# The first projections regrouped: quarters of q, k and v, weights prepared ahead, gated attention's turns

## The chip, the cores and the metric

The kernel runs on one core of one Trainium2 chip. The metric is the device time of one execution in microseconds. Three executions of the kernel before took 2640.57, 2635.28 and 2639.64 us; the median is 2639.64.

## What is computed

The reference is two transformer blocks over 256 tokens of width 2048, all in float32. The diff touches the front of the first block only:

```python
mod = (silu(c) @ ada_w + ada_b)              # 6 x 2048: shift, scale, gate of the mixer and of the ffn
h = rmsnorm(x, norm_mix_g) * (1 + scale_m) + shift_m
(p_q, p_k, p_v, p_g, p_gk, p_cq, p_ckv, p_kr, p_ga, p_gb) = split(h @ w_in)
log_a = log_sigmoid(p_gk @ gla_gk_w + gla_gk_b) / 16
o = gla_chunked(q, k, v, log_a)              # gated linear attention, 4 heads
o = rmsnorm(o, gla_onorm_g) * silu(p_g)
y_gla = o @ gla_wo
# MLA attention from p_cq, p_ckv, p_kr; merged = sigmoid(p_ga) * y_gla + sigmoid(p_gb) * y_mla
```

Then come `w_out`, a gated FFN, and a second block of two layers, none of which the diff touches.

## The kernel before

**Matrix products.** Every weight is read once, in chunks of 128 x 2 x 512 floats (0.524 MB, two tiles of K). A product in float32 is made of three matmuls in fp32r: ScalarE copies the chunk to fp32r (`whi`), VectorE subtracts to get the rest (`wlo`), and TensorE multiplies whi with h's high part, wlo with h's high part and whi with h's low part, in `unit`. Both copies have four slots (`NW`), so the copy of weights chunk w + 4 waits until TensorE is done with chunk w. A product ("job") runs its chunks into one of two pairs of PSUM banks, in turn, and is then read out by `evac`, on ScalarE or VectorE.

**ada_w** doesn't go to TensorE as a matrix: VectorE adds each of its chunks, times a column of silu(c), to `acc` (12 groups of 16 chunks, `adas`). `ada_mod` then sums `acc` over the partitions with 16 one-column matmuls, and VectorE makes the scales `modc`. The mixer's shift and scale come from groups 0 to 3, each for one quarter of the 2048 features.

**The quarters.** h can be made for one quarter of the features when one ada_w group is summed. So q, k and v are computed in four quarters of K, and each later quarter is added to QT, KT or V (`adds`, in `evac` on VectorE, two instructions each). `quarters` in `make_jobs` holds the jobs. Before: in each quarter q and k (two jobs each, 4 tiles of K); v0 in quarter 0, v0 and v1 in quarter 1, and so on, so that a new column block of v starts with each quarter from K = 0. `units` is the order of all chunks: the 16 chunks of ada group 0, then for each of three quarters the 16 chunks of the next ada group, spread evenly, with the quarter's weights in its last 0.8. SP loads the chunks in this order, into 5 slots of raw and, up to here, 6 more (`NFIRST` is 11); each slot is loaded again as soon as VectorE has read it.

**The order of work.** `make_timeline` writes out one list that all engines follow, each picking its own parts. For each chunk of `units` it first emits `prep` for the chunks up to `LOOK` = 3 ahead, ada_w's counted, then the matmuls (`unit`), `evac` at a job's end, and then one step of each running helper stage (`stage_steps`). `until` runs stages on until a named step is out. An engine executes its parts strictly in that order. Stages that matter here: `start` (row sums and norm of X, on ScalarE, VectorE and POOL), `adaf` (`ada_mod`), `fnorm` (`fn_T`, the turn of X on TensorE, with ScalarE's scaling to `hraw`; `fn_hi`, rounding to h's high part on ScalarE and subtraction on VectorE), `tables` (angles, sines), `gk` (the gate's logarithm), `gla` (gated attention: 48 steps of scores, then `gla_av`, 8 products with v, and `gla_og`, 8 steps of turns), `lat` (latents of MLA), `pair` (its heads, two at a time, with softmax). `BORDERS` names jobs before which the tiles of h that they need must be out ahead of any further `prep`.

**The quarters' end.** In quarter 3 the jobs are gk, q, k, v0 to v3; `gla` is launched at v0 and must be out before `ygla` 0.

Of the kernel before, what the change touches and what calls it, by code (L numbers as in the profile page):

```python
# [149 lines left out]
BORDERS = [("fg", 0), ("rvg", 1, 0), ("q", 0, 0), ("q", 0, 1), ("q", 0, 2), ("gk",)]  # L150
# [19 lines left out]
def make_jobs(I):  # L170
# [33 lines left out]
    for qd in range(4):  # L204
        if qd == 3:
            job = gemm("gk", (), lambda k: [(half, sl, cols(w_in, k + 4 * half, o, n, 4)) for half in range(2)
                                            for sl, o, n in ((slice(0, 64), o_kr, 64), (slice(64, 80), o_gk, 16))], KD, 80, "h", turned=True, kn=8)
            quarters[3].append(job)
        for kind, o in (("q", o_q), ("k", o_k)):
            for j in range(2):  # L210
                quarters[qd].append(gemm(kind, (j, qd) if qd < 3 else (j,), wcols(w_in, o + 512 * j, 512), 4, 512, "h", turned=True, k0=4 * qd,
                                         adds=(kind, j, qd - 1) if qd else None))
        for j in range(qd + 1):
            k0 = 0 if j == qd else 4 * qd
            quarters[qd].append(gemm("v", (j, qd) if qd < 3 else (j,), wcols(w_in, o_v + 512 * j, 512), 4 * qd + 4 - k0, 512, "h", k0=k0,
                                     adds=("v", j, qd - 1) if k0 else None))
# [2537 lines left out]
```

## Time and profile before

| | us |
|---|---|
| median of three executions | 2639.64 (2635.28 to 2640.57) |
| span of the profiled execution, first to last instruction | 2637.0 |
| TensorE busy | 2552.6 (97%) |
| VectorE busy | 1699.4 (64%) |
| ScalarE busy | 1281.6 (49%) |

The profile is of one execution; its time is known as its span, and the median of the executions stands 2.6 us above that. PE is TensorE's matmuls, PEld its weight loads, DVE VectorE, ACT ScalarE, POOL GpSimd, SP the engine that issues most loads. `gp` are the PSUM banks of the products, `tp` those of the helper steps. L830, L1270, L1884, L1887 and L1890 are lines of small helpers (matmul, activation, tensor_tensor, tensor_scalar, scalar_tensor_tensor) through which most work is issued, so the tiles tell which step a row belongs to. "x" is a count of instructions; in the rows of groups the mean is that of one instruction.

### The profile page before, as it was taken

Reading aid. Unit: us, or ns where it says so; the run is one execution under the profiler, and the core shown is the slowest. Engines: PE = TensorE matmul, PEld = TensorE weight load, DVE = VectorE, ACT = ScalarE, POOL = GpSimd, SP = SyncE. Lnnn points to the kernel's source line nnn. Section 1 sums busy time; section 2 is a strip of 40 time slices with the busy share of each in tenths; the row PEclk is TensorE's granted clock in tenths of the full one; section 3 lists DMA queues with packets and bytes.
Section 4 is the critical chain, followed back from the end, with each engine's and each line's share of the span. In section 5 each row is a group of like instructions: output and inputs, shape, how many; then the busy total and the mean of one; then the engine's idle time right before and its main releaser. Section 6 shows DMA issues by size and latency. Waiting matters only on the chain.

```text
span 2637.0 us, 33987 instructions
## 1 busy us (share of the span) xinstructions
PE 2552.6 (97%) x12327; PEld 2145.5 (81%) x12327; DVE 1699.4 (64%) x2194; ACT 1281.6 (49%) x1824; POOL 63.1 (2%) x102
## 2 busy tenths in 40 slices
PE   3889999999999999999999999999999999999999
PEld 3878887888887887888888888889888887888887
DVE  6887776776676765566655545565666655676664
ACT  3345455444555444544443444455754545565553
POOL 0000000000000000000000000000000100010000
PEclk9999999999999999999999999999999999999999
DMA  9975665898676665687756666566665465665564
GB/s 364 346 258 152 185 207 183 284 313 269 205 246 200 232 204 187 218 279 253 258 191 194 190 191 190 181 191 181 187 187 172 135 219 147 184 187 180 149 199 135
DMA packets 279920, 555.73 MB, mean 211 GB/s; under 512 B 24286, under 2 KB 45100, under 8 KB 279116
## 3 DMA queue, kind: packets, MB, share of 16 engines
q1 hardware_dynamic: 274048, 541.79, 64.6%
q0 software_dynamic: 3040, 8.69, 1.0%
q10 hardware_dynamic: 2668, 3.09, 0.3%
q8 instruction: 100, 1.64, 0.3%
q14 instruction: 64, 0.52, 0.1%
HBM read 549.83 MB, written 2.10 MB: 209 GB/s over the span
## 4 chain that ended last, share of the span: by engine, by line
PE 91%; DVE 4%; ACT 2%; issue 1%; DMA 1%; SPq 0%; POOL 0%; DVEq 0%; ACTq 0%
PE gp L830 83%; PE tp L830 5%; PE tp L833 2%; DMA raw_first<-in_ada_w_dram 1%; DVE wlo L1884 1%; ACT whi L1270 1%; DVE acc L1890 1%; DVE xs L1884 0%; SPq L813 0%; ACT hraw L1270 0%; DVE stat L2208 0%; ACT sx L1270 0%; DVE sx L1884 0%; DVE yd L1884 0%; ACT h L1270 0%
## 5 line engine op out<-in xcount | busy, mean ns | idle before, releaser
L1884 DVE TENSOR_TENSOR wlo<-raw,whi 128x1024 fp32r<-128x1024 f32 (+1 forms) x830 | 986.0, 1197 | 690.1 <-ACT whi L1270 687.4
L830 PE MATMUL gp<-whi,h 128*128 128x512 f32 (+1 forms) x4352 | 1371.4, 389 | 7.5 <-DVE wlo L1884 4.8
L1270 ACT ACTIVATE whi<-raw 128x1024 fp32r<-128x1024 f32 (+1 forms) x830 | 851.0, 1037 | 666.9 <-PE gp L830 545.6
L830 PEld LDWEIGHTS gp<-whi,h 128*128 128x128 f32 x4352 | 815.6, 188 | 165.9 <-issue 14.0
L830 PE MATMUL gp<-wlo,h 128*128 128x512 f32 (+1 forms) x2176 | 834.8, 384 | 0.0
L830 PEld LDWEIGHTS gp<-wlo,h 128*128 128x128 f32 x2176 | 409.9, 188 | 72.7 <-issue 1.7
L1890 DVE SCALAR_TENSOR_TENSOR acc<-raw,cact,acc 128x1024 f32<-128x1024 f32 x149 | 190.6, 1279 | 7.0 <-DMA raw<-in_ada_w_dram 6.2
L830 PE MATMUL gp<-whi,ah 128*128 128x512 f32 x352 | 137.9, 392 | 0.0
L830 PE MATMUL gp<-whi,al 128*128 128x512 f32 x352 | 137.1, 389 | 0.0
L830 PE MATMUL gp<-wlo,ah 128*128 128x512 f32 x352 | 136.9, 389 | 0.0
L830 PE MATMUL gp<-h,whi 128*128 128x256 f32 (+1 forms) x528 | 106.2, 298 | 20.9 <-ACT whi L1270 10.7
L830 PEld LDWEIGHTS gp<-h,whi 128*128 128x128 f32 (+1 forms) x528 | 87.6, 200 | 25.6 <-issue 16.0
L830 PE MATMUL gp<-whi,mxh 128*128 128x512 f32 x256 | 99.8, 390 | 0.0
L830 PE MATMUL gp<-whi,mxl 128*128 128x512 f32 x256 | 99.6, 389 | 0.0
L830 PE MATMUL gp<-wlo,mxh 128*128 128x512 f32 x256 | 99.6, 389 | 0.0
L830 PE MATMUL gp<-h,wlo 128*128 128x256 f32 (+1 forms) x272 | 79.2, 291 | 0.0
L830 PEld LDWEIGHTS gp<-whi,al 128*128 128x128 f32 x352 | 66.1, 188 | 13.9
L830 PEld LDWEIGHTS gp<-whi,ah 128*128 128x128 f32 x352 | 66.1, 188 | 13.4
L830 PEld LDWEIGHTS gp<-wlo,ah 128*128 128x128 f32 x352 | 66.1, 188 | 13.4
L2603 POOL TENSOR_TENSOR stat<-stat,cst 128x2 f32<-128x2 f32 (+1 forms) x37 | 30.1, 816 | 1436.6 <-DVE stat L1887 1436.4
L1270 ACT ACT_TABLE_LOAD x44 | 56.5, 1283 | 6.2 <-issue 2.9
L830 PEld LDWEIGHTS gp<-wlo,mxh 128*128 128x128 f32 x256 | 48.1, 188 | 10.0
(331 smaller groups left out, 2593.7 us busy)
## 6 DMA issues: line engine op xcount, KB each, us to landing
raw<-in_w_in_dram SPq DMA_DIRECT2D x310, 512.0 KB, 4.3
raw<-in_ffn_w_in_dram SPq DMA_DIRECT2D x176, 512.0 KB, 4.5
raw<-in_ada_w_dram SPq DMA_DIRECT2D x158, 512.0 KB, 4.8
raw<-in_w_out_dram SPq DMA_DIRECT2D x96, 512.0 KB, 4.4
raw<-in_ffn_w_down_dram SPq DMA_DIRECT2D x88, 512.0 KB, 4.3
raw<-in_w_in_dram SPq DMA_DIRECT2D x64, 384.0 KB, 3.3
raw_first<-in_ada_w_dram SPq DMA_DIRECT2D x34, 512.0 KB, 8.4
raw<-in_gla_wo_dram SPq DMA_DIRECT2D x32, 512.0 KB, 5.8
```

The source lines that it names most:

```text
L830: return e.matmul(o, l, r, start=start, stop=stop)
L833: return e.transpose(o, i, ident[0:n, 0:n])
L1270: return e.activation(o, i, f, **kw)
L1884: return e.tensor_tensor(o, a, b, op)
L1890: return e.scalar_tensor_tensor(out=o, in0=a, scalar=s, in1=b, op0=op0, op1=op1)
L2603: e.tensor_tensor(dst, dst, cst[:, C_HALF:C_HALF + n], ALU.pow).then_inc(pow_out, 1)
```

## The change

1. **The quarters.** Quarter 0: q, k over K tiles 0 to 3, v0 over 0 to 3. Quarter 1: no q or k; v1, v2, v3 over tiles 0 to 7. Quarter 2: q, k and v0 over 4 to 11. Quarter 3: v2 over 8 to 15, gk, q and k over 12 to 15, v3 and v1 over 8 to 15, v0 over 12 to 15. 13 partial additions in place of 18. The first halves of v2 and v3 are kept in `VPART`, since X still stands where V will be; `gk_la` waits until v2 is added, since `VPART[2]` lies in LOGA.
2. **The start.** The first two weights chunks stand right behind ada group 0. `x_ss` comes two steps earlier; the turn of X for the first quarter belongs to `start` and precedes `ada_mod`; what ScalarE did in `fn_T` is now `fn_mod`, VectorE's subtraction is `fn_lo`, a step of its own from quarter 1 on. `adaf` 0 and `fnorm` 0 are emitted ahead of the last two ada chunks of group 0. `BORDERS` keeps only the first of the quarters.
3. **Ahead.** From the last chunk of ada group 0 on, `prep` runs to three weights chunks ahead, ada_w's not counted.
4. **The tables** are launched after `fnorm` 3, not 2; `gla` at v3, which is now the first job after k.
5. **Gated attention.** Four of the eight `gla_og` steps stand between the `gla_av` steps, each needing its own head only; `ygla` asks for the tiles that it reads, not for all of `gla`; `lat` needs the last `gla_av` (`GLA_AV`).

```diff
-BORDERS = [("fg", 0), ("rvg", 1, 0), ("q", 0, 0), ("q", 0, 1), ("q", 0, 2), ("gk",)]
+BORDERS = [("fg", 0), ("rvg", 1, 0), ("q", 0, 0)]
+GLA_AV = ("gla", 63)
...
-    for qd in range(4):
...
-        for kind, o in (("q", o_q), ("k", o_k)):
-            for j in range(2):
-                quarters[qd].append(gemm(kind, (j, qd) if qd < 3 else (j,), wcols(w_in, o + 512 * j, 512), 4, 512, "h", turned=True, k0=4 * qd,
-                                         adds=(kind, j, qd - 1) if qd else None))
-        for j in range(qd + 1):
-            k0 = 0 if j == qd else 4 * qd
...
+    qk(0, None, 0, 4)
+    value(0, 0, None, 0, 4)
+    for j in range(1, 4):
+        value(1, j, None, 0, 8)
+    qk(2, 0, 4, 8)
+    value(2, 0, 0, 4, 8)
+    value(3, 2, 1, 8, 8)
...
+    qk(3, 2, 12, 4)
+    value(3, 3, 1, 8, 8)
+    value(3, 1, 1, 8, 8)
+    value(3, 0, 2, 12, 4)
...
-        spots = [((i + 0.5) / 16, 0, u) for i, u in enumerate((adas[qd + 1], ci) for ci in range(KD))]
-        spots += [(0.2 + 0.8 * (i + 0.5) / len(mine), 1, u) for i, u in enumerate(mine)]
+        lead = mine[:2] if qd == 0 else []
+        units += lead
+        mine = mine[len(lead):]
+        spots = [((0.9,1,1)[qd] * (i + 0.5) / 16, 0, u) for i, u in enumerate((adas[qd + 1], ci) for ci in range(KD))]
+        spots += [(0 + (1 - 0) * (i + 0.5) / len(mine), 1, u) for i, u in enumerate(mine)]
...
-        return [idle] * 2 + [step(("x_sq", (), 0)), step(("rows", (), 1))] + [idle] * 4 + [step(("x_ss", (), 0)), idle] + \
-            [step(("x_norm", (t,), 0)) for t in range(2)]
+        return [idle] * 2 + [step(("x_sq", (), 0)), step(("rows", (), 1)), idle, idle, step(("x_ss", (), 0)), idle] + \
+            [step(("x_norm", (t,), 0)) for t in range(2)] + [step(("fn_T", (0,), 1), ("fn_T", (1,), 1))]
...
-        return [step(("fn_T", (2 * j,), 1), ("fn_T", (2 * j + 1,), 1), need=[("start",)]),
-                step(("fn_hi", (2 * j,), 0), ("fn_hi", (2 * j + 1,), 0), *([("gla_loads", (), 0)] if j == 3 else no))]
+        turn = [step(("fn_T", (2 * j,), 1), ("fn_T", (2 * j + 1,), 1))] if j else []
...
-        steps += [step(("gla_av", (h, t), 1), need=[("evac", "v", 3), ("evac", "g", h)]) for h in range(4) for t in range(2)]
-        return steps + [step(("gla_og", (k,), 1)) for k in range(0, KD, 2)]
+        for h in range(4):
+            for t in range(2):
+                turn = [("gla_og", (4 * h + 2 * t - 6,), 1)] if 2 * h + t in (3, 4, 5, 6) else []
+                steps += [step(("gla_av", (h, t), 1), *turn, need=[("evac", "v", 0), ("evac", "g", h)])]
+        return steps + [step(("gla_og", (k,), 1)) for k in range(8, KD, 2)]
...
-                if sid == ("fnorm", 2):
+                if sid == ("fnorm", 3):
                     launch("tables")
...
-        while prep < min(n + LOOK + 1, len(chunks)):
+        ahead = weights_at[n] + LOOK
+        while prep < len(chunks) and (prep <= n + LOOK if n < KD - 1 else prep <= n or weights_at[prep] <= ahead):
...
+        if n == KD - 2:
+            launch("adaf", 0)
+            until(("fnorm", 0))
...
-                if job["name"] == ("ygla", 0):
-                    until(("gla",))
...
-                if job["name"] == ("v", 0):
+                if job["name"] == ("v", 3):
                     launch("gla")
...
+    VPART = {2: w1("vpart2", 0, [2, 512]), 3: w1("vpart3", 42.5, [2, 512])}
...
         def gk_la(us, t):
             for n, u in enumerate(us):
+                w.wait_ge(gp_dve[job_of["v", 2]["no"] % 2], at("gpd", "v", 2))
...
-            for h in range(4):
-                for t in range(2):
-                    taken_dve(first_use("gla_av", h, t))
+            for t in range(2):
+                taken_dve(first_use("gla_av", k // 4, t))
```

## Rows read from the trace of the kernel before

**Rows 1.** The page: span, and busy time of each engine.
```profile
span 2637.0 us, 33987 instructions
PE 2552.6 (97%) x12327; PEld 2145.5 (81%) x12327; DVE 1699.4 (64%) x2194; ACT 1281.6 (49%) x1824; POOL 63.1 (2%) x102
```

**Rows 2.** Busy time by stretch; columns: length, busy, granted clock, DMA share, GB/s.
```profile
0.00:48.80 48.80, 6.36 (x27) 5.42 (x27) 26.88 (x28) 14.55 (x18) 4.97 (x11) 1.00 1.00 356
48.80:83.10 34.30, 31.50 (x219) 29.73 (x219) 27.41 (x24) 12.02 (x16) 0.00 (x0) 1.00 1.05 386
83.10:90.30 7.20, 2.63 (x25) 2.39 (x23) 4.94 (x9) 6.00 (x11) 0.00 (x0) 0.78 1.01 373
90.30:134.20 43.90, 43.70 (x283) 40.09 (x283) 40.52 (x43) 12.47 (x13) 0.00 (x0) 0.96 0.95 329
134.20:152.60 18.40, 11.74 (x81) 11.36 (x79) 13.83 (x28) 10.67 (x16) 0.00 (x0) 0.81 0.68 226
...
48.80:197.20 148.40, 133.75 (x858) 122.46 (x859) 124.85 (x152) 57.89 (x74) 0.00 (x0) 0.95 0.90 313
197.20:300.00 102.80, 99.70 (x589) 86.22 (x587) 76.03 (x99) 52.36 (x71) 0.61 (x2) 0.98 0.55 165
...
700.00:900.00 200.00, 192.09 (x949) 161.37 (x948) 142.79 (x230) 107.55 (x187) 0.96 (x2) 1.00 0.69 221
```

**Rows 3.** TensorE in order of time, start: start us, us, operation, [idle before].
```profile
37.32 3.58 PE L830 MATMUL tp<-cst,acc 128*128 128x1 f32 x16 [17.88 <-DVE acc L1890]
40.76 1.95 PE L833 MATMUL tp<-cst,xs 128*128 128x128 f32 x8
```

**Rows 4.** ScalarE and VectorE in order of time, 33 to 50 us.
```profile
33.69 3.90 ACT L1270 ACTIVATE xs<-xs,stat 128x2048 f32<-128x2048 f32 x2 [12.61 <-POOL stat L2603]
...
38.81 1.29 DVE L1890 SCALAR_TENSOR_TENSOR acc<-raw_first,cact,acc 128x1024 f32<-128x1024 f32 x1 [0.69 <-DMA raw_first<-in_ada_w_dram]
...
42.30 1.28 DVE L1890 SCALAR_TENSOR_TENSOR acc<-raw_first,cact,acc 128x1024 f32<-128x1024 f32 x1 [2.21 <-DMA raw_first<-in_ada_w_dram]
43.51 0.15 DVE L1890 SCALAR_TENSOR_TENSOR modc<-tp,gcol 128x4 f32<-128x4 f32 x1
...
43.90 1.93 ACT L1270 ACTIVATE hraw<-tp,modc 128x256 f32<-128x256 f32 x4 [6.31 <-DVE modc L1884]
...
46.65 1.15 ACT L1270 ACTIVATE h<-hraw 128x512 fp32r<-128x512 f32 x2
...
48.02 1.29 DVE L1884 TENSOR_TENSOR h<-hraw,h 128x512 fp32r<-128x512 f32 x2
```

**Rows 5.** Chain that ended last, 0 to 300 us: start us, us, what.
```profile
48.85 7.82 PE gp L830 x48
...
152.58 8.88 PE gp L830 x72
...
192.64 1.68 PE tp L830 x16
...
239.19 2.73 PE gp L830 x12
```

**Rows 6.** Waits of TensorE, 48.8 to 197.2 us: total, times, longest.
```profile
PE gp L830 <- DVE wlo L1884: 10.0, 8, 5.6
```

**Rows 7.** DMA queues besides SP's, 0 to 200 us: packets, MB, share.
```profile
q10 hardware_dynamic: 2668, 3.09, 4.4%
q0 software_dynamic: 304, 0.66, 0.9%
```

**Rows 8.** VectorE's groups, 48.8 to 197.2 us: count, busy us, mean ns, idle before.
```profile
L1890 DVE SCALAR_TENSOR_TENSOR acc<-raw_first,cact,acc 128x1024 f32<-128x1024 f32 x22 | 28.2, 1280 | 0.3
L1884 DVE TENSOR_TENSOR wlo<-raw_first,whi 128x1024 fp32r<-128x1024 f32 x22 | 26.8, 1221 | 6.8 <-ACT whi L1270 6.8
...
L1884 DVE TENSOR_TENSOR qt<-gp,qt 128x512 f32<-128x512 f32 x8 | 5.1, 684 | 2.3 <-PE gp L830 2.3
```

**Rows 9.** Waits of TensorE, 700 to 900 us: total, times, longest.
```profile
PE gp L830 <- DVE wlo L1884: 4.9, 6, 1.6
```

More of the change, by code:

```diff
@@ L321, in stage_steps @@
         (j,) = args
-        return [step(("fn_T", (2 * j,), 1), ("fn_T", (2 * j + 1,), 1), need=[("start",)]),
-                step(("fn_hi", (2 * j,), 0), ("fn_hi", (2 * j + 1,), 0), *([("gla_loads", (), 0)] if j == 3 else no))]
+        turn = [step(("fn_T", (2 * j,), 1), ("fn_T", (2 * j + 1,), 1))] if j else []
+        last = [("gla_loads", (), 0)] if j == 3 else []
+        return turn + [step(*[(part, (2 * j + n,), 0) for n in range(2) for part in ("fn_mod", "fn_hi")], *([("fn_lo", (2 * j + n,), 0) for n in range(2)] if j == 0 else []), *last)] + \
+            ([step(*[("fn_lo", (2 * j + n,), 0) for n in range(2)])] if j else [])
     if kind == "tables":
@@ L338, in stage_steps @@
             steps += [step(("gla_qk", x, 0), *[("gla_diff", y, 0) for y in ahead]), step(*[("gla_exp", y, 0) for y in ahead]), step(("gla_sc", x, 1))]
-        steps += [step(("gla_av", (h, t), 1), need=[("evac", "v", 3), ("evac", "g", h)]) for h in range(4) for t in range(2)]
-        return steps + [step(("gla_og", (k,), 1)) for k in range(0, KD, 2)]
+        for h in range(4):
[3 more added lines that the diff above has]
+        return steps + [step(("gla_og", (k,), 1)) for k in range(8, KD, 2)]
     if kind == "lat":
         (name,) = args
-        return [idle, idle, idle, step(("lat_T", (name, 0), 1), need=[("gla",)]), step(("lat_T", (name, 2), 1))]
+        return [idle, idle, idle, step(("lat_T", (name, 0), 1), need=[GLA_AV]), step(("lat_T", (name, 2), 1))]
     if kind == "pair":
@@ L471, in stat_need @@
             return [("ffn", k // 2 + 1)]
+        if s == "og":
+            return [("gla", 59 + k // 2)] if k < 8 else [("gla", 60 + k // 2)]
         if s in ("lq", "lk"):
@@ L489, in stat_need @@
         return []
-    prep = 0
+    weights_at, prep = [0], 0
+    for c in chunks:
+        weights_at.append(weights_at[-1] + c["gemm"])
+    late = {1, 2, 3}
     launch("start")
@@ L503, in make_timeline @@
                 was = j["seq"] - (2 if j["seq"] < 4 else 1)
+                if was in late:
+                    late.remove(was)
+                    launch("adaf", was)
                 if was >= 0:
@@ L509, in make_timeline @@
             prep += 1
-        if job["kind"] == "ada" and ci == KD - 1 and job["seq"] < 4:
+        if n == KD - 2:
+            launch("adaf", 0)
+            until(("fnorm", 0))
+        if job["kind"] == "ada" and ci == KD - 1 and job["seq"] in late:
+            late.remove(job["seq"])
             launch("adaf", job["seq"])
@@ L1390, in norm_hi, with fn_mod @@
             note(h_hi, "h", was, pair)
-        def fn_T(us, pair):
+        def fn_mod(us, pair):
             m = first_use("ada_mod", pair // 2)
             w.wait_ge(tp_dve[m.b], at("tpd", *m))
-            norm_T(us[0], pair, hraw, 1, 0, "h")
+            norm_T(first_use("fn_T", pair), pair, hraw, 1, 0, "h")
         def fn_hi(us, pair):
@@ L1762, in evac @@
             elif kind == "v":
-                read(first_use("fn_T", 2 * args[0]))
-                read(first_use("fn_T", 2 * args[0] + 1))
+                j = args[0]
+                if j in VPART:
+                    w.wait_ge(ss_done, at("ss", "x_ss"))
+                else:
+                    read(first_use("fn_T", 2 * j))
+                    read(first_use("fn_T", 2 * j + 1))
                 for n in range(2):
-                    copy(V[:, n, args[0] * 512:(args[0] + 1) * 512], ps[n][:, :]).then_inc(gp_act[g], 1)
+                    copy(VPART[j][:, n, :] if j in VPART else V[:, n, j * 512:(j + 1) * 512], ps[n][:, :]).then_inc(gp_act[g], 1)
             elif kind == "g":
@@ L1987, in norm_lo, with fn_lo @@
             tt(HL[:, kt, :], hr[:, pair % 2, :, :], HH[:, kt, :].bitcast(F32), ALU.subtract).then_inc(h_lo, 1)
-        def fn_hi(us, pair):
+        def fn_lo(us, pair):
             norm_lo(pair, hraw, "h")
@@ L2171, in gla_og @@
             gains()
-            w.wait_ge(ss_done, at("ss", "gla_av", 3, 1))
+            if k >= 8:
+                w.wait_ge(ss_done, at("ss", "gla_av", 3, 1))
             lo_pair(us[0], OGH, OGL, k, [gc(G_ON + (k + n) % 4) for n in range(2)])
@@ L2519, in evac @@
                 if kind == "v":
-                    to = V[:, :, args[0] * 512:(args[0] + 1) * 512]
+                    j = args[0]
+                    to = V[:, :, j * 512:(j + 1) * 512]
+                    if j in VPART:
+                        read(first_use("fn_T", 2 * j))
+                        read(first_use("fn_T", 2 * j + 1))
                     for n in range(2):
-                        tt(to[:, n, :], ps[n][:, :], to[:, n, :], ALU.add).then_inc(gp_dve[g], 1)
+                        tt(to[:, n, :], ps[n][:, :], (VPART[j] if j in VPART else to)[:, n, :], ALU.add).then_inc(gp_dve[g], 1)
                 else:
```

23 lines of the change are left out of this document (12 added, 11 removed).

## The prediction

> **What bounds the kernel now.** I read the page first: TensorE is busy 2552.6 of 2637.0 us [rows 1]. The change issues the same matmuls and transposes on the same operands, so it can win only what the other 84.4 us hold, plus what a throttled clock costs. Then the busy time by stretch [rows 2]: 42.4 us of TensorE's idle time lie before 48.8 us, where the first ada_w group is loaded and the first normed quarter is made; 14.7 us between 48.8 and 197.2, where the quarters of q, k and v run; 3.1 us from there to 300; 7.9 us between 700 and 900, where the pairs of heads run. The rest of the span holds 16.4 us, at places that the diff doesn't touch. In the quarters the mean granted clock is 0.95. Full speed is 2.4 GHz, the lower level half of it, so about a tenth of these 148.4 us ran at half speed: its worst pieces are 83.1 to 90.3 (0.78) and 134.2 to 152.6 (0.81), each just after TensorE had stood idle.
>
> What TensorE waits for in the quarters is prepared weights: ten microseconds for `wlo` in eight places [rows 6]. The two worst places are the borders between quarters. There the last ada_w chunk of the old quarter is summed, TensorE makes its columns (`ada_mod`, 1.68 us [rows 5]), VectorE the scales, TensorE turns X, ScalarE scales and rounds, VectorE subtracts: one chain, with nothing of the new quarter that TensorE could run beside it.
>
> DMA is full in the first quarter, 386 GB/s at a share of 1.05 [rows 2]. It is ahead, though. By 83.1 us it had moved 356 GB/s x 48.8 us + 386 GB/s x 34.3 us = 30.6 MB; 3.75 MB of that are other queues' [rows 7]; 26.9 MB are 51 chunks of 0.524 MB, while TensorE had then used chunk 42. One chunk takes 0.524 MB / 386 GB/s = 1.36 us.
>
> **The change part by part.** *The start.* `x_ss` stands two idle steps earlier, that is two ada_w chunks, at least 2 x 1.36 us: ScalarE's norm of X ends at 34.9 at the latest instead of 37.6 [rows 4]. TensorE's turn of X (1.95 us [rows 3]) then ends by 36.9, ahead of `ada_mod` (37.32, 3.58 us [rows 3]), where today it follows it. Two weights chunks stand behind ada group 0, and VectorE does their `wlo` before the scales. Chunk 17 was there at 38.81 [rows 4]; copy and subtraction of it end near 41.0, the end of `ada_mod` too. From there 0.4 us of scales (43.51 to 43.90), 1.93/2 of `hraw`, 1.15/2 of `h`, 1.29/2 of the subtraction [rows 4]: first matmul at 43.8 instead of 48.85, a gain of 5.0. If chunk 17 lands as late as chunk 18 did (42.30 [rows 4]) it is 47.3, a gain of 1.5.
>
> *Quarter 0.* 8 chunks of q and k at 8.88/3 = 2.96 us and 2 of v at 2.73 [rows 5] are 29.1 us; the first two ran at the low clock and took 7.82 instead of 5.92 [rows 5], which I keep: 43.8 + 29.1 + 1.9 = 74.8. Its last chunk (index 41) lands at 83.1 - 9.2 x 1.36 = 70.6, in time.
>
> *Quarter 1* now is v1 to v3 alone over 8 tiles of K: 12 chunks of v, 16 of ada_w, no partial addition. TensorE needs 12 x 2.73 + 1.68 + 1.0 (two turns at full speed, an estimate from half of 1.95) = 35.4 us, VectorE 16 x 1.28 + 12 x 1.22 = 35.1 [rows 8], DMA 28 x 1.36 = 38.1. So DMA sets the end: chunk 69 lands at 83.1 + 18.8 x 1.36 = 108.7; copy, subtraction and 2.73 of matmuls make it 113.6. The border is covered by two chunks of v1 that need only the first normed quarter. VectorE's scales stand behind every chunk prepared ahead (through index 50, which lands at 82.5), so normed tiles come at 86, TensorE is there at 83.3 and waits 2.7 us; supply hides that.
>
> *Quarter 2* has 8 tiles of K for q, k and v0: 16 x 2.96 + 4 x 2.73 = 58.3 us of TensorE for 36 chunks, 49.0 us of DMA: TensorE sets the pace. At its border the scales wait behind index 77 (119.6), the normed tiles come at 123.5, TensorE is there at 122.1: 1.4 us. 113.6 + 1.7 + 1.0 + 58.3 + 1.4 = 176.0. For the clock after these waits I add 1.7 us, about half of what 134.2 to 152.6 lost (18.4 x 0.19). The quarters end at 177.7 where they now end at 197.2: **-19.5**, of which the start is a quarter. Ends of this term: with no wait, TensorE's work alone, 171.0 (-26); with the start at 47.3, DMA at 329 GB/s as from 90.3 to 134.2 [rows 2] and both border costs as now, -10. I stay near the first: in the stretch before it DMA gave 386 GB/s, and nothing is added to what it must bring.
>
> *Five partial additions fewer.* Each is two instructions of 0.684 us [rows 8], 6.8 us of VectorE. I cost them at nothing by themselves: the VectorE time of quarter 1 above is already without them, and supply is slower. Without that cover they would be worth 6.8 us at most. Quarter 3 now has eight additions for seven; 1.4 us of VectorE, hidden by 24 chunks of TensorE.
>
> *The tables* (some 6 us of VectorE) are launched a quarter later. They now sit in the worst stretch, 134.2 to 152.6; in quarter 3 VectorE is busy 76.0 of 102.8 us [rows 2]. The steps of gk stand behind them, and `gk_la` also waits on ScalarE for the addition of v2, with the copies of weights queued behind it; but v2 was added some four chunks before, and gla starts only with v3, eight chunks of q and k after gk. SP's queue carries the same loads in the new order, POOL's the same steps (its loads for gla still stand with the last normed quarter). **0**, from -4 (the 3.1 us idle and the clock of 0.98 go) to +3 (the wait moves there).
>
> *Three weights chunks ahead, ada_w's not counted.* Before, an ada_w chunk among the next three leaves two weights chunks, 5.5 us of cover. Where chunks alone fill the ring nothing changes. Between 700 and 900 bursts of VectorE and ScalarE work for the softmax hold back `wlo`: 4.9 us in six waits, none over 1.6 [rows 9]. A further chunk covers 2.1 to 2.8 us, more than any of them. **-4**, of 7.9 idle; from -7 to +3, since the softmax's own steps now stand behind one more chunk.
>
> *Gated attention turned as it ends.* Eight turns of 4 transposes each move from behind the last `gla_av` to between them, and ygla no longer waits for all of gla. TensorE does the same work, and the stretch after 197.2 shows next to no idle time outside those named. **0**, +-1.
>
> Sum: -19.5 - 4 = -23.5 on a span of 2637.0, 2613.5; the median run is 2.6 us above the span, which I keep: **2616.1**.
>
> **The skill against a row.** DMA moved 386 GB/s over 34 us [rows 2]. The Trainium skill, "DMA: Bandwidth & Descriptors", section Specifications, puts HBM's limit for a core at about 358 GB/s. By it 70 chunks and 3.75 MB are there at 113.0 us, quarter 1 ends at 117.9, and the sum is 2620.4; the row says that a core which runs alone gets more.
>
> **The rivals.** (1) *The supply is later than I count* (0.17): the weights of v1 to v3 arrive behind ada_w chunks, quarter 1 stalls as the borders do now, and the clock falls. For it: slack of 0 to 3 us on three resources at once in quarter 1. Against it: DMA was nine chunks ahead. That is the -10 end, with -2 elsewhere: 2627. The skill's limit, above, is a mild form of it. (2) *All of it comes through* (0.12): -26 and -7, 2606. (3) *Slower: helper steps too late* (0.06). Between 300 and 900 each ScalarE or VectorE step of gla and of the pairs now stands behind the preparation of a third weights chunk, which waits for the slot that TensorE just left. If a pair's chain pays for this twice, 8 pairs x 2 x 2.1 us = 34 us come back: 2650. It decides from the point where such a step takes longer than the two chunks (5.5 us) that are left ahead of TensorE. Against it: stretches without ada_w work this way already, and at the present spacing TensorE waits little there for anything but `wlo`. (4) *Nothing in the end* (0.09): the quarters finish earlier, but gla, whose first steps wait for k, the tables and the gate, then sets the pace before v is done: 2637. Against it: gla's start keeps its distance from gk, and TensorE has ten chunks of quarter 3 and all of g beside it.
>
> **How the numbers follow.** Forecast 0.56, at 2616 (2609 to 2624 with the bounds of its terms). Range 2605 to 2632: it takes in the forecast, (1) and most of (2). A measurement of this kernel tells 0.2%, 5 us, from no change. Faster: the forecast, (1), (2), 0.85; same: (4), 0.09; slower: (3), 0.06.
>
> **What would show it.** First gp matmul at 43 to 45 us. No stretch of the quarters with a clock below 0.9, and no idle piece of TensorE over 3 us in them. The last `ada_mod` of the quarters near 173 instead of 192.64 [rows 5]. 700 to 900, counted from its own start, with 3 to 5 us idle. Wrong if the first matmul is at 47 or later, if quarter 1 ends after 118, if the profile shows TensorE waiting for `tp` steps of the pairs by over 5 us in sum, or if the gain before gla is given back before ygla.

## The result, and the profile after

The changed kernel takes 2614.39 us (median; 2612.94 to 2616.49), the kernel before beside it 2639.77: a ratio of 0.9909, 95% interval 0.9897 to 0.9921. The forecast was 2616, within 2605 to 2632. The total is right to 1.6 us. Its terms aren't: they miss by up to 5 us and cancel. Of one version below, the changed kernel without the look-ahead, one execution of four was in a slow state (3225.19 us, at a mean clock of 0.753), and its times are those of the other three.

The page of the changed kernel, as in [rows 1]: span, and busy time of each engine.

```profile
span 2614.7 us, 34013 instructions
PE 2546.4 (97%) x12327; PEld 2142.6 (82%) x12327; DVE 1697.4 (65%) x2184; ACT 1289.7 (49%) x1824; POOL 62.2 (2%) x102
```

TensorE has the same 12327 matmuls, VectorE ten instructions fewer. Lines L861 and L864 are now the matmul helper, L1300 ScalarE's, L1919, L1922 and L1925 VectorE's. The span fell by 22.3 us, the median by 25.4. The difference lies in which execution was profiled: each of the changed kernel's four takes 1.8 us more than its own span, and the profiled one (2616.49) is the slowest of them. So the median stands 0.3 us below the profiled span, where before it stood 2.6 above.

Busy time by stretch, as in [rows 2] (length, then PE, PEld, DVE, ACT, POOL busy, granted clock, DMA share, GB/s). The first three are quarter 0, quarter 1, and the time until TensorE has done 792 matmuls into `gp`, a count that [rows 2]'s kernel reached at 197.2.

```profile
46.30:82.00 35.70, 33.93 (x241) 32.31 (x242) 32.69 (x29) 14.95 (x20) 0.00 (x0) 1.00 1.05 386
82.00:119.70 37.70, 34.44 (x147) 28.01 (x145) 34.60 (x34) 18.74 (x25) 0.00 (x0) 0.95 1.05 387
119.70:182.70 63.00, 62.61 (x482) 60.51 (x481) 50.61 (x54) 29.36 (x35) 0.00 (x0) 1.00 0.85 295
...
700.00:900.00 200.00, 196.20 (x963) 165.00 (x962) 142.15 (x220) 108.92 (x180) 0.96 (x2) 1.00 0.68 221
```

The stretches with a clock near 0.8 have no like here: up to matmul 792 the clock is low once, for 3.4 us from 91.3, where before it was low twice for 6.8 (from 87.1 and 138.3). But three resources are now close to full in quarters 0 and 1 at once: TensorE idles 1.8 and 3.3 us, VectorE is busy 32.7 of 35.7 and 34.6 of 37.7 us (27.4 of 34.3 in quarter 0 before), and DMA stands at a share of 1.05 for 73 us. ScalarE shows what that means: between 46 and 182 us it waits for DMA in 22 places.

Waits of ScalarE in the changed kernel, 46 to 182 us (total, times, longest):

```profile
ACT whi L1300 <- DMA raw_first<-in_w_in_dram: 24.1, 12, 3.7
ACT whi L1300 <- DMA raw<-in_w_in_dram: 17.5, 10, 4.3
```

TensorE in order of time, the idle pieces over 0.33 us from 34 to 240 us (start, us, operation, [idle before]); [rows 3] shows the first two of before.

```profile
34.01 1.97 PE L864 MATMUL tp<-cst,xs 128*128 128x128 f32 x8 [14.83 <-ACT xs L1300]
38.25 3.54 PE L861 MATMUL tp<-cst,acc 128*128 128x1 f32 x16 [2.27 <-DVE acc L1925]
46.30 0.55 PE L861 MATMUL gp<-h,whi 128*128 128x256 f32 x1 [4.50 <-DVE h L1919]
...
65.94 0.36 PE L861 MATMUL gp<-h,whi 128*128 128x256 f32 x1 [0.35 <-DVE wlo L1919]
...
69.66 0.35 PE L861 MATMUL gp<-h,whi 128*128 128x256 f32 x1 [0.61 <-DVE wlo L1919]
...
73.57 0.47 PE L861 MATMUL gp<-whi,h 128*128 128x512 f32 x1 [0.80 <-DVE wlo L1919]
...
90.74 0.47 PE L861 MATMUL gp<-whi,h 128*128 128x512 f32 x1 [3.26 <-DVE h L1919]
...
128.62 0.36 PE L861 MATMUL gp<-h,whi 128*128 128x256 f32 x1 [0.39 <-DVE h L1919]
...
223.91 0.39 PE L861 MATMUL gp<-h,whi 128*128 128x256 f32 x1 [2.46 <-DVE qt L1919]
```

The two border waits of the kernel before, which [rows 6] don't tell apart:

```profile
90.34 0.55 PE L830 MATMUL gp<-h,whi 128*128 128x256 f32 x1 [4.60 <-ACT whi L1270]
...
140.61 0.55 PE L830 MATMUL gp<-h,whi 128*128 128x256 f32 x1 [5.59 <-DVE wlo L1884]
```

The turn stands ahead of `ada_mod` as foretold, at 34.01 instead of 40.76 [rows 3]; the first product starts at 46.30 instead of 48.85 [rows 5]. Of the borders between the quarters one wait of size is left in this profile, at 90.74; a second profile of the same kernel, below, has two of about 2 us. The last `ada_mod` of the quarters runs at 174.5, where it ran at 192.64 [rows 5].

To place the gain I counted TensorE's matmuls into `gp` in both traces and compared when each count is reached. At the first product the changed kernel is 2.6 us ahead; at the 792nd (197.2 before, 182.7 now) 14.5; after gated attention (1900 matmuls) 16.9; after the pairs (3400) 22.3, and about as much at the end. So: **quarters with the start -14.5, quarter 3 and gated attention -2.4, pairs -5.4**. Below, "at matmul 792" is this count.

### The profile page after: what moved, and what is told of

It reads as the page before. It is cut to its first block, busy times and chain, and to the rows that moved or that the text cites. A ratio compares the mean times of both kernels' runs of the same rounds, so it can differ in the third digit from the quotient of the medians.

```text
span 2614.7 us, 34013 instructions
## 1 busy us (share of the span) xinstructions
PE 2546.4 (97%) x12327; PEld 2142.6 (82%) x12327; DVE 1697.4 (65%) x2184; ACT 1289.7 (49%) x1824; POOL 62.2 (2%) x102
## 4 chain that ended last, share of the span: by engine, by line
PE 87%; DVE 2%; ACT 1%; issue 1%; POOL 0%; DVEq 0%; ACTq 0%
PE gp L861 79%; PE tp L861 5%; PE tp L864 2%; DVE wlo L1919 0%; ACT whi L1300 0%; DVE xs L1919 0%; DVE stat L2244 0%; DVE yd L1919 0%; ACT sx L1300 0%; DVE rg L1925 0%; DVE sx L1919 0%; DVE sx L1922 0%; DVE st L1919 0%; ACT mxh L1300 0%; DVE stat L1922 0%
## 5 line engine op out<-in xcount | busy, mean ns | idle before, releaser
L1919 DVE TENSOR_TENSOR wlo<-raw,whi 128x1024 fp32r<-128x1024 f32 (+1 forms) x828 | 987.0, 1197 | 703.5 <-ACT whi L1300 700.7
L861 PE MATMUL gp<-whi,h 128*128 128x512 f32 (+1 forms) x4352 | 1368.4, 389 | 7.1 <-DVE h L1919 4.9
L1300 ACT ACTIVATE whi<-raw 128x1024 fp32r<-128x1024 f32 (+1 forms) x828 | 854.3, 1036 | 770.7 <-PE gp L861 705.9
L861 PEld LDWEIGHTS gp<-whi,h 128*128 128x128 f32 x4352 | 815.5, 188 | 160.8 <-issue 10.8
L861 PE MATMUL gp<-wlo,h 128*128 128x512 f32 (+1 forms) x2176 | 834.5, 384 | 0.0
L861 PEld LDWEIGHTS gp<-wlo,h 128*128 128x128 f32 x2176 | 410.0, 188 | 72.7 <-issue 1.2
L1925 DVE SCALAR_TENSOR_TENSOR acc<-raw,cact,acc 128x1024 f32<-128x1024 f32 x150 | 191.9, 1279 | 7.8 <-DMA raw<-in_ada_w_dram 6.7
L861 PE MATMUL gp<-whi,ah 128*128 128x512 f32 x352 | 138.0, 392 | 0.0
L861 PE MATMUL gp<-whi,al 128*128 128x512 f32 x352 | 137.1, 389 | 0.0
L861 PE MATMUL gp<-wlo,ah 128*128 128x512 f32 x352 | 137.0, 389 | 0.0
L861 PE MATMUL gp<-h,whi 128*128 128x256 f32 (+1 forms) x528 | 103.7, 294 | 8.5 <-DVE h L1919 4.9
L861 PE MATMUL gp<-whi,mxh 128*128 128x512 f32 x256 | 99.8, 390 | 0.0
L861 PE MATMUL gp<-whi,mxl 128*128 128x512 f32 x256 | 99.7, 389 | 0.0
L861 PE MATMUL gp<-wlo,mxh 128*128 128x512 f32 x256 | 99.6, 389 | 0.0
L861 PEld LDWEIGHTS gp<-h,whi 128*128 128x128 f32 (+1 forms) x528 | 85.6, 196 | 12.4 <-issue 8.3
L861 PE MATMUL gp<-h,wlo 128*128 128x256 f32 (+1 forms) x272 | 78.3, 288 | 0.0
L861 PEld LDWEIGHTS gp<-whi,al 128*128 128x128 f32 x352 | 66.1, 188 | 13.9
L861 PEld LDWEIGHTS gp<-wlo,ah 128*128 128x128 f32 x352 | 66.1, 188 | 13.5
L861 PEld LDWEIGHTS gp<-whi,ah 128*128 128x128 f32 x352 | 66.1, 188 | 13.4
L861 PEld LDWEIGHTS gp<-wlo,mxh 128*128 128x128 f32 x256 | 48.1, 188 | 10.0
```

Source lines behind the costliest of these rows:

```text
L861: return e.matmul(o, l, r, start=start, stop=stop)
L1300: return e.activation(o, i, f, **kw)
L1919: return e.tensor_tensor(o, a, b, op)
L1925: return e.scalar_tensor_tensor(out=o, in0=a, scalar=s, in1=b, op0=op0, op1=op1)
```

## The experiments

The one-part versions come first, then the disputed costs, then what follows for a better kernel. Ratios are to the kernel before. No run turns back the new start alone, nor one part of the diff that neither the list of the change nor the forecast names: the new `spots` spread a quarter's weights over all of it, no longer over its last 0.8.

**Look-ahead alone, on the kernel before.**

```diff
-        while prep < min(n + LOOK + 1, len(chunks)):
+        ahead = weights_at[n] + LOOK
+        while prep < len(chunks) and (prep <= n + LOOK if n < KD - 1 else prep <= n or weights_at[prep] <= ahead):
```

> The kernel before with one part of the change alone: from the last chunk of ada group 0 on, three weights chunks are prepared ahead, ada_w's not counted. Theory (three separate gains: the start 2.5 us, the covered borders and the new quarters some 14, the pairs 5): only the 0.6 to 0.8 us waits for wlo at job ends in the first quarter and the wlo waits between 640 and 940 us go, so 5 to 8 us under the kernel before, some 2632; no wait for wlo is left in the pairs, the two borders stay. Rival (looking further ahead is what counts, the regrouping is only a rearrangement): 17 us or more under, 2623 or less.

Measured: 2636.51 us, ratio 0.9995 (0.9986 to 1.0004): nothing that can be told from no change, and less than either theory had. Yet in its trace two things of opposite sign happened. In the pairs it gains 6.8 us by the count of matmuls. At the front it loses 10.5 us by the 96th matmul, 5.9 at matmul 792. ScalarE, VectorE and TensorE of this kernel, each in order of time, about its first product:

```profile
54.78 1.06 ACT L1273 ACTIVATE whi<-raw_first 128x1024 fp32r<-128x1024 f32 x1 [3.01 <-DMA raw_first<-in_w_in_dram]
...
57.08 0.15 DVE L1893 SCALAR_TENSOR_TENSOR modc<-tp,gcol 128x4 f32<-128x4 f32 x1
...
60.78 0.55 PE L833 MATMUL gp<-h,whi 128*128 128x256 f32 x1 [17.55 <-DVE h L1887]
```

`ada_mod` was done at 41.4, but the scales (`modc`) stand in VectorE's queue behind every chunk that is prepared ahead; the last of these landed at 54.78. So the look-ahead makes the chain longer at the start, and at the first border too (a wait of 6.14 us, before 4.60), but not at the second (5.41, before 5.59). It pays here only with the new start and the new jobs at the borders, which the next version shows from the other side.

**The changed kernel without the look-ahead.** The same line, turned back.

```diff
-        while prep < len(chunks) and (prep <= n + LOOK if n < KD - 1 else prep <= n or weights_at[prep] <= ahead):
+        while prep < min(n + LOOK + 1, len(chunks)):
```

> The changed kernel with the old look ahead (three chunks, ada_w's counted). Theory: the pairs lose their 5 us again, and in quarters 0 to 2 the waits for wlo come back in part, 1 to 4 us: 2620 to 2624; TensorE waits for wlo by some 5 us in the pairs. Rival (looking ahead counts for most): 2632 or more.

Measured: 2626.55, ratio 0.9956 (0.9939 to 0.9972), 12.2 us above the changed kernel, 9.5 by the span: between the theories. The old waits for `wlo` are back; waits of TensorE in this kernel, 46 to 190 us, then 700 to 900:

```profile
PE gp L860 <- DVE wlo L1918: 8.0, 8, 3.5
```
```profile
PE gp L860 <- DVE wlo L1918: 3.5, 4, 1.6
```

At matmul 792 it is 5.0 us behind the changed kernel, after gated attention 6.7, after the pairs 10.0. So the look-ahead gives 5 us in the quarters, 1.7 in quarter 3 and gated attention (2.6 in the experiment before this one), 3.3 in the pairs. What I put down to the regrouping is to a third the look-ahead's. In the pairs this kernel is still 2.0 us ahead of the kernel before, without the look-ahead; no run shows why.

**The changed kernel with the old quarters.** 18 additions, v column by column as before; start, look-ahead and turns as changed.

```diff
-    qk(0, None, 0, 4)
-    value(0, 0, None, 0, 4)
-    for j in range(1, 4):
-        value(1, j, None, 0, 8)
...
+    for qd in range(4):
+        for kind, o in (("q", o_q), ("k", o_k)):
...
+        for j in range(qd + 1):
```

> The changed kernel with the old quarters of q, k, v (18 partial additions, each quarter beginning with a chunk of q that needs the tiles normed last), everything else as changed. Theory: the borders are bare again, two to three of them at some 5 us of idle time and 2 to 3 us of low clock each: 10 to 15 us over the changed kernel, 2625 to 2630, with idle pieces of 4 us or more where quarters 1 and 2 begin. Rival (regrouping is worth nothing once weights are further ahead): within 3 us of the changed kernel, 2612 to 2618.

Measured: 2622.95, ratio 0.9942 (0.9927 to 0.9957): 8.6 us above the changed kernel, 5.6 by the span, 7.6 at matmul 792: again between the two. TensorE at its two borders:

```profile
87.76 0.55 PE L851 MATMUL gp<-h,whi 128*128 128x256 f32 x1 [6.29 <-DVE h L1908]
...
136.03 0.55 PE L851 MATMUL gp<-h,whi 128*128 128x256 f32 x1 [3.89 <-DVE h L1908]
```

Here q's first chunk needs the new normed quarter at once; in the changed kernel two chunks of v1 stand ahead of it. At each the clock was low for 6.8 us. These two places are where the trace shows the regrouping's gain, 5.6 to 8.6 us in all. (The spread of `spots` stayed as changed.)

**The five additions put back as bare VectorE time.** Ten 128 x 512 additions into a spare tile at the ends of v1, v2 and v3 of quarter 1; nothing else is touched.

```diff
+            if kind == "v" and len(args) == 2 and args[1] == 1:
+                w.wait_ge(d_first, at("first"))
+                w.wait_ge(mm_done, job["chunks"][-1]["w"] + 1)
+                for n in range(4 if args[0] < 3 else 2):
+                    tt(SPARE[:, :], cst[:, 0:512], cst[:, 512:1024], ALU.add).then_inc(dve_self, 1)
+                    w.wait_ge(dve_self, own())
+                return
```

> The changed kernel with the VectorE time of five partial additions put back: ten additions of 128 x 512 floats into a spare tile, 6.8 us in all, where the jobs of quarter 1 end (four behind v1, four behind v2, two behind v3). Nothing of the result hangs on them. Theory (the additions cost nothing by themselves): within 1.5 us of the changed kernel, 2613 to 2616. Rival (VectorE sets the pace of quarter 1, so its five additions fewer are the gain there): 5 to 7 us more, 2619 to 2621.

Measured: 2620.08, ratio 0.993 (0.9914 to 0.9947): 5.7 us above the changed kernel, 3.8 by the span, 3.5 at matmul 792. "Nothing by themselves" is wrong: the median lies in the rival's range, the trace below it. In this kernel, VectorE's spare additions from 85 to 130 us, and TensorE:

```profile
L1920 DVE TENSOR_TENSOR spare<-cst 128x512 f32<-128x512 f32 x10 | 6.9, 690 | 0.2
```
```profile
118.64 0.47 PE L862 MATMUL gp<-whi,h 128*128 128x512 f32 x1 [1.86 <-DVE wlo L1920]
...
132.09 0.36 PE L862 MATMUL gp<-h,whi 128*128 128x256 f32 x1 [2.06 <-DVE h L1920]
```

6.9 us of VectorE (idle for only 0.2 us ahead of them) in a stretch where it had 3.1 us to spare come out as two waits, 3.9 us together. Where I had taken nothing, they cost about half their time by the trace, in two profiles whose clock fell once each up to matmul 792 (against the repeat below, whose clock didn't fall, it is 5.1 us), and four fifths by the medians.

**The old turns of gated attention.**

```diff
-        for h in range(4):
-            for t in range(2):
-                turn = [("gla_og", (4 * h + 2 * t - 6,), 1)] if 2 * h + t in (3, 4, 5, 6) else []
...
+        return steps + [step(("gla_og", (k,), 1)) for k in range(0, KD, 2)]
```

> The changed kernel with gated attention's turns as before: all eight behind the last product with v, each waiting for all eight products, and ygla waiting for all of gla. Theory (the turns are TensorE's own work wherever they stand, and there is other work beside them): within 1.5 us of the changed kernel, 2613 to 2616; the stretch from quarter 3 to the first product of uq as long as in the changed kernel, within 0.8 us. Rival (the 2.6 us that the change gained between the end of quarter 2 and uq are the turns'): 2 to 3 us more, 2616.5 to 2617.5.

Measured: 2614.17, ratio 0.9904, span 2614.7. **The tables launched as before:**

```diff
-                if sid == ("fnorm", 3):
+                if sid == ("fnorm", 2):
                     launch("tables")
```

> The changed kernel with the tables launched when the third normed quarter is done, as before, not the fourth. Theory (some 6 us of VectorE come into quarter 2, where TensorE sets the pace, and leave quarter 3, where the gate's chain holds an addition of q back by 2.5 us): -2 to +2 us against the changed kernel, 2612 to 2616.5. Rival (moving the tables is worth the 2.6 us gained between quarter 2 and uq): 2 to 4 us more, with a new idle piece of over 1 us in quarter 2.

Measured: 2613.99, span 2613.0. Neither part's worth can be told from nothing, as forecast. The second shows more: the wait of 2.5 us in quarter 3 (222.21 there) doesn't come from the tables. ScalarE and VectorE of the changed kernel ahead of 223.91:

```profile
215.82 1.06 ACT L1300 ACTIVATE whi<-raw 128x1024 fp32r<-128x1024 f32 x1 [5.29 <-DMA raw<-in_w_in_dram]
216.90 1.28 ACT L1300 ACT_TABLE_LOAD   x1
218.19 2.19 ACT L1300 ACTIVATE loga<-loga,cst 128x1024 f32<-128x1024 f32 x2
...
221.43 1.23 DVE L1919 TENSOR_TENSOR wlo<-raw,whi 128x1024 fp32r<-128x1024 f32 x1 [0.83 <-ACT whi L1300]
222.57 1.28 DVE L1919 TENSOR_TENSOR qt<-gp,qt 128x512 f32<-128x512 f32 x2
```

ScalarE waited 5.29 us for the chunk of 215.82; the gate's table load and logarithm follow on ScalarE, the next copy stands behind them, and the addition of q, for whose banks TensorE waits, stands behind that copy's subtraction. As these rows read, the price sits in the order of the queues; no run changed that order.

**Scales one chunk earlier.** The prediction's start failed at the chunks that VectorE must subtract ahead of the scales. Here only one of them is left.

```diff
-        if n == KD - 2:
+        if n == KD - 3:
             launch("adaf", 0)
```

> The changed kernel with the first scales and the first normed quarter emitted one ada chunk earlier, so that VectorE has one weights chunk, not two, in front of them. Theory (the first matmul waits for the second of those two chunks, which landed at 41.06 us): first product at 45.0 instead of 46.3 us, and since quarter 1 waits for VectorE later anyway, 0 to 1.3 us less in all, 2613 to 2614.5. Rival (the first weights chunk itself is late, so that nothing changes, or the second one then is): first product at 46 or later, 2614 to 2616.

Measured: 2613.86; first product:

```profile
44.27 0.55 PE L861 MATMUL gp<-h,whi 128*128 128x256 f32 x1 [3.37 <-DVE h L1919]
```

2.0 us earlier than in the changed kernel. 0.9 of it isn't the edit's: the last ada_w chunk of group 0 came earlier in this execution, and `ada_mod` began at 37.35 instead of 38.25. The other 1.1 are the second chunk's. At matmul 792 the kernel is 1.7 us ahead of the first profile of the changed kernel and level with its repeat (below).

**v1 and v2 interleaved at the border of quarter 1**, so that four chunks, not two, need no new normed tile.

```diff
+        if qd == 1:
+            mine = [mine[i] for i in (0, 1, 4, 5, 2, 3, 6, 7, 8, 9, 10, 11)]
```

> The changed kernel with the chunks of quarter 1 in the order v1, v1, v2, v2 (first normed quarter), v1, v1, v2, v2 (second), then v3, so that four chunks and not two need no newly normed tile. Theory (TensorE's 3.3 us of idle time and the low clock behind it, 1.7 us, come from those scales standing on VectorE behind the chunks prepared ahead): no idle piece over 1 us and no low clock where quarter 1 begins, 2 to 5 us less, 2609.5 to 2612.5. Rival (VectorE sets the pace of quarter 1, so what isn't waited for there is waited for later): within 1.5 us of the changed kernel, with a new idle piece at the border to quarter 2.

Measured: 2615.69, ratio 0.9912. The wait at that border is gone, and one at the next has come:

```profile
126.93 0.36 PE L863 MATMUL gp<-h,whi 128*128 128x256 f32 x1 [2.71 <-DVE h L1921]
```

TensorE ended quarter 1 at 115.8, 0.7 us ahead of the repeat below, but the scales of the next border came no earlier (the product there starts at 126.93, in the repeat at 126.96), mostly as the rival had it. If cover helps, both borders need it.

**Half of ada_w's loads left out.** Groups 1 and 2 (those of quarters 0 and 1) are loaded half; all engines work as before.

```diff
-"src": [(slice(0, 512), src[k * P:(k + 1) * P])]
+"src": [(slice(0, 256), src[k * P:(k + 1) * P, :, 0:256]) if seq in (1, 2) else (slice(0, 512), src[k * P:(k + 1) * P])]
```

> The changed kernel, but the chunks of ada_w that stand in quarters 0 and 1 (groups 1 and 2) are loaded only half (256 of each 512 columns); the rest of the slot keeps old data, so these scales are not the reference's. VectorE, ScalarE and TensorE do all their work as before; 8.4 MB of 21 in these quarters are not moved. It tells whether the supply or VectorE sets the waits of quarters 0 and 1 in the changed kernel. Supply (my theory for quarter 0): the waits of 0.35 to 0.8 us in quarter 0 go, quarter 0 ends 1.5 to 2 us earlier, ScalarE's waits for DMA (24.1 us there) nearly go; at the border to quarter 1 VectorE is early too; the quarters end 4 to 6 us earlier, 2608 to 2611. Rival (VectorE, 92% busy in quarter 1, sets it): the quarters end within 1.5 us of the changed kernel, 2612.5 to 2615.

**Cover at both borders** (and the scales one chunk earlier):

```diff
-        if n == KD - 2:
+        if n == KD - 3:
...
+        if qd:
+            mine = [mine[i] for i in (0, 1, 4, 5, 2, 3, 6, 7)] + mine[8:]
```

> The changed kernel with the first scales emitted one ada_w chunk earlier, and with the jobs at both inner borders interleaved (v1 and v2 in quarter 1, the two q jobs in quarter 2), so that four chunks, not two, need only normed tiles that are there. Theory: the waits at the borders are a matter of cover; first product at 44.3 us, no idle piece over 1 us at either border, 4 to 6 us off: 2608.5 to 2611. Rival: supply and VectorE take back what the cover gives, some wait follows within the same quarter: 2612 to 2615.

**The changed kernel once more, beside these two.**

> The changed kernel itself once more, beside the two others on the same chip, as their yardstick: 2613 to 2616, first product at 46.3 us, border waits of 2 to 3.5 us where they fell before or at the next border.

Measured: half loads 2611.51 (0.9899; 0.9886 to 0.9913), cover at both 2612.04 (0.9900; 0.9887 to 0.9914), the changed kernel again 2615.47 (0.9913; 0.9900 to 0.9927). The repeat's waits at the two borders, then all waits of TensorE with half loads, 40 to 140 us, and its windows 46.3 to 82 and 82 to 119.7, the times of the changed kernel's quarters 0 and 1:

```profile
89.03 0.47 PE L861 MATMUL gp<-whi,h 128*128 128x512 f32 x1 [1.88 <-DVE h L1919]
...
126.96 0.36 PE L861 MATMUL gp<-h,whi 128*128 128x256 f32 x1 [2.08 <-DVE h L1919]
```
```profile
PE gp L861 <- DVE h L1919: 5.5, 2, 4.7
PE gp L861 <- DVE wlo L1919: 1.1, 2, 0.6
...
46.30:82.00 35.70, 34.62 (x244) 33.06 (x244) 34.56 (x31) 17.16 (x23) 0.00 (x0) 1.00 0.90 285
82.00:119.70 37.70, 36.84 (x182) 30.96 (x181) 37.28 (x39) 19.23 (x25) 0.00 (x0) 1.00 0.99 341
```

Half loads: neither theory whole. ScalarE's waits for DMA between 46 and 182 us fall from 41.6 us to 3.9, yet quarter 0 keeps two of its waits for `wlo` (0.47 and 0.61): with the data there, VectorE is busy 34.6 of 35.7 us and is the next limit. My theory for quarter 0 falls. At the borders it holds: the first wait shrinks to 0.86 (4.7 of the 5.5 is the start's) and the second is gone; the quarters reach matmul 792 at 177.6, against 181.1 in the repeat and 182.7 in the first profile. Supply is worth 3.5 us against the repeat, whose clock didn't fall up to there either, by the scales' and copies' queues; behind it VectorE has nothing left (37.3 of 37.7 us).

Cover at both borders: no idle piece over 0.7 us from 46 to 219 us, and matmul 792 at 178.4. The borders are as the theory said, the time isn't: it lies 3.4 us below the repeat in the median and 2.8 in the span, at the edge of the rival's range. The first product came at 45.26, not 44.3, and quarter 0 has four waits of 0.4 to 0.6 us, which take part of it back. It is the lowest of the kernels here that compute everything. The two intervals overlap, but each of its four executions (2609.69 to 2612.74) lies below each of the nine of the changed kernel (2612.94 to 2616.90), so a small gain is likely.

## Why the prediction came out, by its own steps

**The start: mis-sized.** Gain 2.55, not 5.0. ScalarE, then VectorE of the changed kernel, as in [rows 4]:

```profile
39.70 1.06 ACT L1300 ACTIVATE whi<-raw_first 128x1024 fp32r<-128x1024 f32 x1 [5.75 <-DMA raw_first<-in_w_in_dram]
41.06 1.06 ACT L1300 ACTIVATE whi<-raw_first 128x1024 fp32r<-128x1024 f32 x1 [0.30 <-DMA raw_first<-in_w_in_dram]
...
40.86 2.58 DVE L1919 TENSOR_TENSOR wlo<-raw_first,whi 128x1024 fp32r<-128x1024 f32 x2 [2.76 <-ACT whi L1300]
43.36 0.15 DVE L1925 SCALAR_TENSOR_TENSOR modc<-tp,gcol 128x4 f32<-128x4 f32 x1
```

The step took chunk 17's landing from before, 38.81 [rows 4]; it landed at 41.06. From the end of its subtraction to the first product the forecast had 2.8 us (the items that it names add up to 2.6), measured 2.9. Only the landing failed, inside the bounds given (43.8 to 47.3). One chunk fewer ahead of the scales leaves 3.0 to 3.4 us between the end of `ada_mod` and the first product (two kernels) instead of 4.5.

Why the landing moved can be read from the traces. POOL issues loads of its own behind its step of the norm, 0.66 MB [rows 7], or 1.7 us at 386 GB/s. Its load of `lv`, in the kernel before and in the changed one:

```profile
33.61 0.70 POOL L2620 DMA_DIRECT2D lv<-const_lvl_dram  x1
```
```profile
31.12 0.57 POOL L2660 DMA_DIRECT2D lv<-const_lvl_dram  x1
```

Before, these loads moved between 37.7 and 41.8 us, and chunk 18 landed 3.5 us behind chunk 17. With `x_ss` earlier, they moved between 34.0 and 38.6, and it was chunk 16 that landed late, 2.9 us behind chunk 15; elsewhere a chunk follows in about 1.36 us. So the edit that brought the norm forward also put POOL's loads in front of the two weights chunks. The forecast had POOL's steps as unchanged. No run moves these loads alone.

**Quarter 0: a limit left out.** Forecast end 74.8. TensorE reached the end of its jobs, with the next `ada_mod` (1.7) already among them, at 81.1: 2.5 us from the start, 1.7 from that place, 1.8 from three waits for `wlo`, 0.3 elsewhere. The 1.9 us that the forecast keeps for a low clock in the first two chunks stand in no row as a granted clock (1.00 in [rows 2]; the trace's first entry of the clock is at 52.96), but in the pace: in both kernels TensorE started 19 matmuls in the first 4 us of the products and 32 or 33 in the next 4. I had costed this quarter by TensorE's work and by one landing. VectorE was counted only for quarter 1, but in quarter 0 it is full too: 16 ada_w additions (10.3 + 10.3 us) and ten `wlo` (7.3 + 4.9) in the 35.7 us, as the groups show.

VectorE's groups, 46.3 to 82 us, as in [rows 8]:

```profile
L1925 DVE SCALAR_TENSOR_TENSOR acc<-raw_first,cact,acc 128x1024 f32<-128x1024 f32 x8 | 10.3, 1282 | 0.4
L1925 DVE SCALAR_TENSOR_TENSOR acc<-raw,cact,acc 128x1024 f32<-128x1024 f32 x8 | 10.3, 1282 | 0.4
L1919 DVE TENSOR_TENSOR wlo<-raw_first,whi 128x1024 fp32r<-128x1024 f32 x6 | 7.3, 1222 | 1.2 <-ACT whi L1300 1.1
L1919 DVE TENSOR_TENSOR wlo<-raw,whi 128x1024 fp32r<-128x1024 f32 x4 | 4.9, 1220 | 0.3 <-ACT whi L1300 0.3
```

**Landings.** The forecast divided bytes moved by the size of a chunk. The rate was right (386 and 387 GB/s), the landing not: chunk 41, forecast for 70.6, was copied at 75.08, as soon as it came. Chunk 41 was issued at 63.29, and eight others landed between then and its own landing, so the bytes moved hold parts of chunks of which none is whole. In the kernel before, chunk 48 landed at 83.08: 49 chunks were whole where the forecast counted 51. That is 2.2 chunks, 3.0 us, and so much smaller was the slack of "nine chunks ahead".

The other 1.7 us are this execution's. The copy of chunk 29 in it, then in the repeat:

```profile
59.01 1.06 ACT L1300 ACTIVATE whi<-raw_first 128x1024 fp32r<-128x1024 f32 x1 [3.72 <-DMA raw_first<-in_w_in_dram]
```
```profile
57.17 1.06 ACT L1300 ACTIVATE whi<-raw_first 128x1024 fp32r<-128x1024 f32 x1 [2.00 <-DMA raw_first<-in_w_in_dram]
```

It landed 3.0 us behind chunk 28 here and 1.35 in the repeat, with DMA at 383 and 384 GB/s meanwhile, and every later chunk up to the border lands 1.7 us later than in the repeat. Rival (1), supply later than counted, was so in part what happened: half loads gave 3.5 us back.

**Quarter 1.** Forecast end 113.6, measured 119.8 (116.5 in the repeat); the sign "wrong if quarter 1 ends after 118" came true in the first profile and not in the second, and the other three signs of being wrong in neither. The border wait was foretold at 2.7 and was 3.26 (1.88 in the repeat). The chain there is as described, with two slips: the scales stand behind fewer chunks than I said (index 47, not 50, since ada_w chunks aren't prepared past the last weights chunk), and the supply enters once more, on ScalarE.

ScalarE of the changed kernel at this border:

```profile
87.24 1.06 ACT L1300 ACTIVATE whi<-raw_first 128x1024 fp32r<-128x1024 f32 x1 [2.03 <-DMA raw_first<-in_w_in_dram]
88.20 1.00 ACT L1300 ACTIVATE hraw<-tp,modc 128x256 f32<-128x256 f32 x2
```

The scales were out at 85.8; `hraw` had to stand behind a copy whose chunk landed at 87.24. In the repeat that chunk was copied at 85.53, and the wait is shorter by 1.4 us. The claim "supply hides that" failed: the wait of TensorE at the border wasn't made good later; that VectorE at 92% had no room to run ahead is argued, not shown. The two runs with more cover agree: cover at one border moved the wait to the next; cover at both took out waits of 4.0 us in sum and is 2.6 us ahead of the repeat at matmul 792, of which 0.9 is the earlier start.

The prediction's reading of [rows 6] has a slip of its own: of the two border waits of before, only the second (5.59) is among the ten microseconds for `wlo`; the first (4.60) stands under `whi`, in a row that [rows 6] leave out.

**Quarter 2.** Border wait forecast 1.4; measured 0.39, in the repeat 2.08. TensorE then does set the pace (62.6 of 63.0 us). **The quarters in all**: 182.7 against 177.7, -14.5 against -19.5, inside the term's ends (-26 to -10).

**The five additions**: "nothing by themselves" failed; the experiment gives 3.5 to 3.8 us by the trace, 5.7 by the medians, for 6.9 us of VectorE. The cover named, supply, hid half of it at most.

**The tables and the turns**: 0 and 0, as forecast.

**The look-ahead in the pairs**: forecast -4, from -7 to +3. Waits of TensorE, 700 to 900 us, as in [rows 9]:

```profile
PE tp L861 <- ACT qrt L1300: 2.2, 3, 1.1
PE tp L864 <- DVE sx L1922: 1.3, 2, 0.9
```

`wlo` is gone from the list, and the softmax's steps stand where they stood: 3.8 us idle in 200, within the 3 to 5 foretold. The term came to -5.4, between the 3.3 and 6.8 us of the two experiments on it. Rival (3), helper steps too late, didn't happen in the pairs. Its mechanism did happen elsewhere: in the kernel before with the look-ahead alone, the further chunks stood ahead of the scales and cost 5.9 us by matmul 792.

**Not in the sum**: -2.4 between matmul 792 and 1900, about what the look-ahead is worth there (1.7 and 2.6 in the two experiments on it). The bounds given for the tables hold it, but the tables aren't its cause.

**Sum and median.** By the span the errors are +5.0, -1.4 and -2.4: 2614.7 against 2613.5. The forecast added 2.6 for the median, as before; but 1.8 of that is what an execution takes beyond its span, and the rest was which execution had been profiled. Now the median lies 0.3 under the profiled span, so the total came out 1.6 too high. The sum's closeness is mostly luck of signs; the bounds of the terms, on which the range rested, held.

**The Trainium skill against the row.** DMA held 386 to 387 GB/s from 46.3 to 119.7 us. The trace doesn't agree with the limit of about 358 GB/s that the Trainium skill gives for a core ("DMA: Bandwidth & Descriptors", section Specifications). The time that I had worked out from it for the end of quarter 1, 117.9, lies between the two profiles' 116.5 and 119.8, but for other reasons: waits at the border and VectorE, at a rate that the rows show to be higher.

**"No clock below 0.9, no idle piece over 3 us" in the quarters**: wrong for the profile, with one piece of 3.26 and the clock low for 3.4 us behind it; right in the repeat.

## What to carry to other kernels

When an edit packs the work closer, add up each engine's work in each stretch afresh, not only the engine that set the pace before: VectorE at 80% in quarter 0 became a limit at 92%, and additions that looked free in quarter 1, at 92% too, cost half their time or more. Preparing further ahead and the order at a border are one decision, since whatever is prepared ahead stands in the same queues in front of the chain that opens the next stretch. Take a chunk's time of arrival from the row where its first user waits for it, not from bytes divided by a rate, and look which other loads an edit moves in front of it.

## What the runs showed of the hardware

The same wait of TensorE is sometimes followed by a low clock and sometimes not. In quarter 3 it waits 2.45 or 2.46 us in the changed kernel, its repeat and seven of the other versions. Behind it the clock fell to half in five of these nine profiles and stayed up in four, the repeat among them. Windows of 3.5 us right after it, in the changed kernel and its repeat:

```profile
224.30:227.80 3.50, 3.50 (x19) 3.50 (x19) 3.47 (x7) 1.06 (x1) 0.61 (x2) 0.51 0.56 149
```
```profile
222.30:225.80 3.50, 3.50 (x32) 3.50 (x31) 3.46 (x7) 1.06 (x1) 0.62 (x2) 1.00 0.52 153
```

A clock of 0.5 is 1.2 GHz instead of 2.4: 19 matmuls instead of 32 in the same time; half speed for 3.4 us costs some 1.7. With half loads it was 0.52 there, with cover at both borders 1.00. The two profiles of the changed kernel differ by 1.7 us at matmul 792: in one a chunk landed late, a border wait of 3.26 us followed and the clock fell behind it (then 0.39 at the next border); in its repeat the waits are 1.88 and 2.08, and the clock stayed up. So differences under 2 us at that place between the last five kernels aren't read as gains of their edits, unless the clock fell equally often in both.
